# A decoder trunk in three-pass fp32r: two down-projections of each feed-forward stage turned from direct products into seven half-size products, and two of the four weight sums made by adding DMAs

## The reference, cut to what matters

```python
def swiglu_half(h, g, w1, w3, w2):
    u = rmsnorm(h, g)
    return h + 0.5 * ((jax.nn.silu(u @ w1) * (u @ w3)) @ w2)

def decoder_layer(h, ...):
    h = swiglu_half(h, *ffn1)
    h, sd, sq, sc = hybrid_mixer(h, s_delta, s_qkv, s_conv, n_lead, *mixp)
    h = swiglu_half(h, *ffn2)
    return h, sd, sq, sc
```

## Time and profile before

| | |
|---|---|
| median of 3 runs | 1204.9 us |
| the profiled execution | 1204.62 us |
| its span, first to last instruction | 1202.6 us |
| TensorE busy, matmuls | 1190.0 us (99%), 8832 |
| VectorE busy | 788.3 us (66%) |
| ScalarE busy | 515.5 us (43%) |
| POOL busy | 76.5 us (6%) |
| granted TensorE clock, mean | 0.997 of full speed |
| moved by DMA | 99.68 MB, mean 83 GB/s |

### The profile page before, as it was taken

How to read it: one execution, slowest core, us unless ns; L and a number is a source line. 1 busy time by engine, 2 the same in 40 slices (tenths; PEclk the granted TensorE clock), 3 DMA queues, 4 the chain that set the end, 5 groups by cost and what they waited for, 6 DMA issues and landing times.

```text
span 1202.6 us, 21067 instructions
## 1 busy us (share of the span) xinstructions
PE 1190.0 (99%) x8832; PEld 1162.1 (97%) x8832; DVE 788.3 (66%) x1155; ACT 515.5 (43%) x820; POOL 76.5 (6%) x58
## 2 busy tenths in 40 slices
PE   9999999999999999999999999999999999999997
PEld 9999999999999998999989898999999999999997
DVE  6887565767566633766557787547776667675764
ACT  6345343435344532433443444443344344353355
POOL 0000000000000300000125210220000000000003
PEclk9999999999999999999999999999999999999999
DMA  5321212221212422211510002422133121222112
GB/s 191 128 87 72 105 62 97 89 105 71 106 71 105 117 95 70 67 57 54 122 9 1 1 2 88 132 70 89 53 116 124 69 97 63 97 106 105 71 71 79
DMA packets 39212, 99.68 MB, mean 83 GB/s; under 512 B 12112, under 2 KB 15568, under 8 KB 39120
## 3 DMA queue, kind: packets, MB, share of 16 engines
q1 hardware_dynamic: 38064, 96.00, 23.4%
q10 hardware_dynamic: 1056, 2.36, 0.5%
HBM read 92.91 MB, written 5.44 MB: 82 GB/s over the span
## 4 chain that ended last, share of the span: by engine, by line
PE 92%; issue 3%; DVE 2%; ACT 1%; POOL 1%; DMA 0%; POOLq 0%; DVEq 0%; SPq 0%
PE ps L846 34%; PE ps L813 21%; PE ps L762 19%; PE ps L958 10%; PE ps L1349 4%; PE ps L726 1%; PE ps L1155 1%; PE ps L1363 1%; ACT x_hi L1431 1%; DVE w_lo L1926 1%; DVE h L1988 1%; PE ps L928 0%; PE ps L982 0%; PE ps L1261 0%; DMA h<-x_t 0%
## 5 line engine op out<-in xcount | busy, mean ns | idle before, releaser
L846 PE MATMUL ps<-x_hi,s_hi 128*128 128x296 f32 (+1 forms) x576 | 171.2, 297 | 0.2
L846 PE MATMUL ps<-x_hi,s_lo 128*128 128x296 f32 (+1 forms) x576 | 170.9, 297 | 0.0
L846 PE MATMUL ps<-x_lo,s_hi 128*128 128x296 f32 (+1 forms) x576 | 170.9, 297 | 0.0
L762 PE MATMUL ps<-x_hi,w_hi 128*128 128x296 f32 (+1 forms) x608 | 136.1, 305 | 0.3 <-DVE x_lo L1931 0.3
L762 PE MATMUL ps<-x_lo,w_hi 128*128 128x296 f32 (+1 forms) x608 | 131.8, 298 | 0.0
L762 PE MATMUL ps<-x_hi,w_lo 128*128 128x296 f32 (+1 forms) x608 | 131.7, 298 | 0.0
L846 PE MATMUL ps<-t_hi,s_hi 128*128 128x296 f32 (+1 forms) x432 | 128.3, 297 | 0.0
L846 PE MATMUL ps<-t_hi,s_lo 128*128 128x296 f32 (+1 forms) x432 | 128.1, 297 | 0.0
L846 PE MATMUL ps<-t_lo,s_hi 128*128 128x296 f32 (+1 forms) x432 | 128.0, 296 | 0.0
L2025 DVE TENSOR_TENSOR s_lo<-s_sum,s_hi 128x1024 fp32r<-128x1024 f32 x72 | 88.2, 1225 | 43.0 <-ACT s_hi L1418 40.3
L846 PEld LDWEIGHTS ps<-x_hi,s_hi 128*128 128x128 f32 x576 | 108.4, 188 | 0.6 <-issue 0.6
(11 more groups left out here) (322 smaller groups left out, 2556.4 us busy)
## 6 DMA issues: line engine op xcount, KB each, us to landing
raw<-weights SPq DMA_DIRECT2D x150, 512.0 KB, 3.3
raw<-weights SPq DMA_DIRECT2D x16, 384.0 KB, 3.5
S<-states SPq DMA_DIRECT2D x1, 2048.0 KB, 11.8
new_state<-S ACTq DMA_DIRECT2D x1, 2048.0 KB, 6.9
y_t<-h SPq DMA_DIRECT2D x4, 336.0 KB, 2.3
h<-x_t SPq DMA_DIRECT2D x4, 296.0 KB, 5.0
h<-x_t SPq DMA_DIRECT2D x2, 592.0 KB, 7.0
raw<-weights SPq DMA_DIRECT2D x4, 256.0 KB, 5.3
```

Of the source, the lines that this page charges most:

```text
L762: last = nc.tensor.matmul(ps[:, slot if out is None else out, half, 0:w_half], w[:, slot, k, :], x[:, k, a:a + w_half], start=(k == 0 and ...
L846: last = nc.tensor.matmul(out, w[:, k, :], x[:, k, :], start=(start and k == 0 and r == 0), stop=(k == KT // 2 - 1 and r == 2), skip_group ...
```

## The change: what it does

1. `PARTS` is `[4, 4, 4, 3, 3, 4]`. The parts of four tiles that are neither first nor last, parts 1 and 2 of each stage, are `split`.
2. The down-projection of a split part is done by the same seven products. A pair `j` of 0 to 3 is one 2 by 2 block product: two output tiles (2j, 2j+1) from two times two hidden tiles, with token halves as columns. One pair is seven products of 2 k-steps, 42 matmuls. The weights of pairs 0 and 1 are one use of the piece set (`pair_uses[0]`), those of pairs 2 and 3 the other (`pair_uses[1]`).
3. It needs T1 to T4 of the hidden tiles: tiles 0 and 1 keep their second token half aside and give T1; tiles 2 and 3 give T3, T2, T4 (`gt_sums`), each cast (`gt_cast`) and with its rest (`gt_rest`, `rests`).
4. `h` takes from each pair three adds in place of two: M7 alone on both halves, the rest of the second row, the first row.
5. S3 and S1 are no longer made on VectorE. SP loads one block in their place (`load_bases`) and POOL issues a DMA that adds the other block to it (`add_bases`, `accum_op=ALU.add`). S3 and S1 and what follows change sign, so the adds to `h` have -0.5.
6. In the mixer the first `w` of `ORDER` moves behind one step of `a` and two of `s`, `hist_q` is loaded after the masks, some semaphores are merged, and rows of `work` are 8 columns longer.

```diff
-PARTS = [4, 4, 3, 3, 4, 4]
+PARTS = [4, 4, 4, 3, 3, 4]
...
+        self.split = n == 4 and 0 < at < len(PARTS) - 1
...
-    "aabaabbsatazsaabaazbaabaabscaabtabasbaabsababaasbsstaassaaacansasaswasssshhhwssshww"
+    "aabaabbsatazsaabaazbaabaabscaabtabasbaabsababaasbsstaassaaacansasasasswsshhhwssshww"
...
+            def load_bases(t):                                   # SP
+                for i, at in enumerate((S3, S1)):
+                    sum_free(sp, t, at)
+                    if t.w or i:
+                        sp.wait_ge(base_in, 32 * t.w + 16 * i)
+                    sp.dma_start(piece(2, t.use, at), weights[t.u + 1][:, 0:KT // 2]).then_inc(base_in, 16)
...
+            def add_bases(stage):                                # POOL
+                for part in FFN[stage][1:]:
+                    for t in part.tiles + part.pair_uses:
+                        for i, (at, j, k) in enumerate(((S3, 0, 0), (S1, 1, KT // 2))):
+                            pool.wait_ge(base_in, 32 * t.w + 16 * (i + 1))
+                            if t.w or i:
+                                pool.wait_ge(base_sums, 32 * t.w + 16 * i)
+                            pool.dma_start(piece(2, t.use, at), weights[t.u + j][:, k:k + KT // 2],
+                                           accum_op=ALU.add).then_inc(base_sums, 16)
...
++            def down_sevenths(part):                             # TensorE
+                pair_m1(part, 1)
+                for j in range(2):
+                    for product_of in (pair_m7, pair_m6, pair_m2):
+                        product_of(part, j, (0,))
+                pair_m7(part, 0, (1,))
+                pair_m6(part, 0, (1,))
+                pair_m2(part, 0, (1,))
+                pair_m5_m4(part, 0)
+                pair_m7(part, 1, (1,))
+                pair_m6(part, 1, (1,))
+                pair_m2(part, 1, (1,))
+                pair_m3(part, 0)
+                pair_m5_m4(part, 1)
+                pair_m1(part, 2)
+                pair_m7(part, 2)
+                pair_m3(part, 1)
+                pair_m6(part, 2)             # waits for S2 of the second pair use, hi and lo
+                pair_m2(part, 2)
+                pair_m5_m4(part, 2)
+                pair_m1(part, 3)
+                pair_m7(part, 3)
+                pair_m3(part, 2)             # waits for pair_rest_add(2)
+                pair_m6(part, 3)
+                pair_m2(part, 3)
+                pair_m5_m4(part, 3)
+                m1(FFN[part.stage][part.at + 1].tiles[0])
+                pair_m3(part, 3)
...
+            def down_sevenths(part, lo):                         # ScalarE
+                hi_first(second)
+                pair_seed("b", part, 1)
+                first_casts(t, lo)
+                last_casts(t, lo)
+                pair_seed("c", part, 0)
+                hi_sums(second, 0)
+                pair_seed("c", part, 1)
+                hi_sums(second, 1)
+                hi_last(second)
+                pair_seed("b", part, 2)
+                hi_first(after)
+                pair_seed("c", part, 2)
+                hi_sums(after, 0)
+                pair_seed("b", part, 3)
+                hi_sums(after, 1)
+                pair_seed("c", part, 3)
+                seed(after)
+                hi_last(after)
...
+            def gt_sums(t, lo):                                  # VectorE
+                dve.wait_ge(halves_out, half_out("product", t.t))
+                dve.wait_ge(g_ready, G_DONE["T1", t.part.tiles[j].abs])
+                V.tensor_tensor(t3, b22, t3, ALU.subtract).then_inc(halves_out, 1)
+                V.scalar_tensor_tensor(t2, t2, -1.0, b22, ALU.mult, ALU.subtract).then_inc(halves_out, 1)
+                dve.wait_ge(halves_out, half_out("T2", t.t))
+                V.scalar_tensor_tensor(t4, t2, -1.0, b21, ALU.mult, ALU.subtract).then_inc(halves_out, 1)
...
+            def down_sevenths(part, lo):                         # VectorE
+                rests(t, lo)
+                lo_first(second)
+                pair_m7_add(part, 0)
+                pair_rest_add(part, 0)
+                sum_two(second)
+                lo_sums(second, 0)
+                pair_add(part, 0)
+                pair_m7_add(part, 1)
+                pair_rest_add(part, 1)       # waits for d4 of pair 1
+                sum_four(second)
+                lo_sums(second, 1)           # waits for the cast of S2 with S4
+                pair_add(part, 1)
+                lo_last(second)
+                lo_first(after)
+                pair_m7_add(part, 2)
+                sum_two(after)               # waits for the adding DMAs of the next part's first tile
+                pair_rest_add(part, 2)
+                lo_sums(after, 0)
+                sum_four(after)
+                pair_add(part, 2)
+                pair_m7_add(part, 3)
+                lo_sums(after, 1)
+                pair_rest_add(part, 3)
+                pair_add(part, 3)
+                lo_last(after)
```

More of the change, by code:

```diff
@@ L77, in __init__, with pair @@
         self.uses = 0 if at == 0 else n + 2
+        self.pair_uses = [PairUse(self, i) for i in range(2)] if self.split else []
+    def pair(self, j):
+        return self.stage, self.at, j
     def tile(self, i):
@@ L106, in __init__, with split_number @@
         self.use = part.use + i
+        self.w = split_number(part) + i
         self.last = i == part.n - 1
+class PairUse:
+    def __init__(self, part, i):
+        self.part, self.i = part, i
+        self.u = part.down + 2 * i
+        self.use = part.use + part.n + i
+        self.w = split_number(part) + part.n + i
+def split_number(part):
+    sizes = [n + 2 * (n == 4 and at < len(PARTS) - 1) for at, n in enumerate(PARTS) if at]
+    return part.stage * sum(sizes) + sum(sizes[:part.at - 1])
 def ffn_parts(stage):
@@ L666, in load_parts @@
                     for t in part.tiles:
-                        load_used(part, t.u, t.use, KT)
-                    for i in range(2):
+                        for load in (load_bases, load_tile) if t.use == 1 else (load_tile, load_bases):
+                            load(t)
+                    for x in part.pair_uses:
+                        load_tile(x)
+                        load_bases(x)
+                    for i in range(0 if part.split else 2):
                         load_used(part, part.down + 2 * i, part.use + part.n + i, 2 * part.n)
@@ new lines, in pair_m3, with down_sevenths @@
+            def pair_m3(part, j):
+                pe.wait_ge(halves_out, half_out("rest", part.pair(j)))
+                pair_seventh(part, j, S4, "B22", "c", False).then_inc(unit_done, part.step(2 * j) + part.step(2 * j + 1))
+            def down_sevenths(part):
+                pair_m1(part, 1)
+                for j in range(2):
+                    for product_of in (pair_m7, pair_m6, pair_m2):
[23 more added lines that the diff above has]
+                pair_m3(part, 3)
@@ L1524, in by_sevenths @@
                     hi_sums(nxt, 1)
-                    seed(nxt)
+                    if t.last:
+                        pair_seed("b", part, 0)
+                    else:
+                        seed(nxt)
                     hi_last(nxt)
@@ L2048, in by_sevenths @@
                 part, lo = t.part, lo_of(t.part.stage)
-                nxt = None if t.last else part.tiles[t.i + 1]
+                nxt = following(t)
                 if t.i:
```

400 lines of the change are left out of this document (330 added, 70 removed).

## The result

| | before | changed |
|---|---|---|
| median (4 runs each, side by side) | 1204.79 us | 1238.93 us |
| lowest to highest | 1204.36 to 1205.02 | 1237.25 to 1242.89 |
| ratio, 95% interval | | 1.0283 [1.0262, 1.0305] |
| profiled execution, its span | 1204.62, 1202.6 us | 1240.19, 1238.4 us |

The change makes the kernel 34 us slower. The forecast was 1205.6 us in a range of 1199 to 1218; the time lies outside it, on the side of rival 1.

The account below looks back on a forecast made before the run. TensorE, never idle in the feed-forward windows, was taken as the bound. Matmuls saved -12.9 us and new waits +13.6 net +0.7: 1204.6 becomes 1205.3, 1205.6 as a median; eight-in-ten range 1199 to 1218 us.

Parts of the forecast that it names:

- rival 1: Adding DMAs land late, x above 3.7 us, VectorE waits in `sum_two`; x of 4 to 5 gives 1208 to 1222; chance 0.32.
- 96 matmuls fewer: Four split down-projections, two per stage, each drop 24 matmuls, at 0.1359 and 0.1326 us each: 12.9 us saved.
- The waits of the split parts' own queues: TensorE's new waits for VectorE and ScalarE in split parts: 3.4 us a part, 13.6 for four.
- A: Split down-projection: m6 of pair 2 waits for S2, behind pair 1's rest add, sum, cast and rest: 2.0 us lost.
- B: m1 of pair 1, first product after the last tile's m4, waits for that tile's SiLU on ScalarE: 0.5 us lost.
- C: k-step 1 of pair 0 waits for T3 and g of the last tile: 0.5 us lost together.
- D: m5 of pair 3 waits for a seed behind ScalarE's cast of 1024 for the next part: 0.3 us lost.
- POOL is held up by a busy VectorE: GpSimd writes DMA descriptors in SBUF, and VectorE's two-port modes lock it out: 0.25 us or so a time.
- x: Time of one adding DMA from POOL's release to its semaphore: taken as 3.3 us, bounded by 2.7 and 5.3.
- 2.7 + 2x <= 10.1: Split part's end: a load and two serial adds must fit before the next part's `sum_two`; x up to 3.7 us.
- the forecast's own case: Adds in time, split parts lose 3.0 to 4.2 us each: net -0.9 to +3.9 us; chance 0.40.
- The moved `w`: Mixer, near 740 us: 1.06 us of ScalarE and 1.2 of VectorE move elsewhere; -1 to +1, taken as 0.

Follow-up runs that it names:

- experiment 1: Changed kernel without the 88 adding DMAs, SP's base load giving their signal (additions left out): 1209.77 us, ratio 1.0037 to the kernel before.
- experiment 5: experiment 1 with VectorE and ScalarE making S2 and S4 of the second pair use before waiting for pair 1: 1199.58 us, ratio 0.9952.
- experiment 9: Experiment 7 with S2 and S4 sums ahead of the activation rests in tiles 1 to 3 of split parts: 1198.61 us, ratio 0.9952.
- experiment 4: Changed kernel with POOL's 88 DMAs as plain copies in series, without the addition (sums left out): 1210.26 us, ratio 1.005.
- experiment 10: Changed kernel, adds in series, each covering only the first half of its block, 128 KB (other half left out): 1214.16 us, ratio 1.01.
- Experiment 7: Changed kernel with both adds of a use in flight, `w` back in place, and S2 and S4 made earlier in split down-projections: 1201.42 us, ratio 0.9978.
- experiment 3: Changed kernel with separate semaphores, so a use's two base loads and two adds no longer wait for each other: 1211.33 us, ratio 1.0059.

## Why the prediction was wrong

**What held.** 96 matmuls fewer, at the pitch of the earlier trace rows: starts on time follow each other after 0.136 us in stage 0 and 0.133 in stage 1 in both kernels, and the experiments that take the waits away shorten the stages. The waits of the split parts' own queues: 13.6 forecast, 13.1 measured in experiment 1, and not by chance, since they agree place by place: A 2.0 (2.0 forecast), B 0.4 to 0.5 (0.5), C 0.6 (0.5), D 0.15 to 0.3 (0.3). Chain A's four ops took 3.73 us (3.86). A and B are also shown by the edits that remove them, experiments 5 and 9; C and D were not tested apart.

**What did not.** The forecast would be wrong by much "if TensorE stands in the middle of tiles". It does: 9.3 us at L1009 for ScalarE, the largest row of its waits. VectorE at the end of a split part (134 to 160 us) is busy 20.7 of 26 us, 80% and not near 90%. And the reason for late adds that POOL is held up by a busy VectorE shows nowhere in POOL's issues: they took 0.865 us at the median and 1.01 at most over all 88.

**The step that failed: x.** "It reads 256 KB twice, so I take the row of 512 KB, 3.3." That was a row of SP's queue used for POOL's. Measured, x is 5.1 us at the median, near the upper bound of the text: POOL's 0.86 us of issuing, then some 4.2 until it is released. The plain copy of experiment 4 shows how it is made up: a transfer of this size on POOL's queue is already 4.1 with no addition (3.6 to landing, against 2.8 from SP); the addition brings 1.0 more, 0.33 of it on POOL. How much of the copy's time is due to the loads beside it no run here separates. The condition, 2.7 + 2x <= 10.1, was the right one, and rival 1 named place, mechanism and what would show it: VectorE in `sum_two` for a DMA, x from POOL's row. It was given 0.32 where the forecast had 0.40, and the range was cut at x = 4.9.

By the Trainium skill (DMA: Bandwidth & Descriptors, "Anatomy of one DMA") a DMA that GpSimd issues takes 2.0 us and its bytes at 436 GB/s, 2.6 for 256 KB; here the plain copy took 3.6 us to landing and 4.1 to the next release, the add 4.7 and 5.1. The measurement decides, and it was also the page's figure that made a value near 3.3 look safe.

**The second miss: the slope.** Even with x right the forecast would have been too low. For x = 5.3 the text had about +21 us over the forecast's own case, some 19 for 5.1. The changed kernel's waits are 20.6 + 24.8 = 45.4; less 13.1 of experiment 1 and 3.4 of granted clock (below) the late adds cost 28.9. It is also steeper: at x = 4.1 they cost 0.5 (experiment 4 against 1), or 4.4 in experiment 10, where the text had +3 to +4. The loss feeds itself: the use after the late one starts its load late too, and load, add, add took 16.6 us where the text had 11.8, with base loads of 5.0 and 3.8 us in the chain in place of 2.7. I had laid out the first late tile, not the loop.

**The moved `w`.** Taken as 0 (-1 to +1); it costs 2.0. In the changed kernel's mixer TensorE stands for the rest of that split:

```profile
760.13 1.22 DVE L2254 TENSOR_TENSOR w_lo<-raw,w_hi 128x1024 fp32r<-128x1024 f32 x1
...
761.40 0.53 PE L1523 MATMUL ps<-xoc_hi,w_hi 128*128 128x288 f32 x2 [1.97 <-DVE w_lo L2254]
```

ScalarE's cast of 1.04 us and VectorE's rest of 1.22 now lie behind two steps that TensorE waits for in turn, where one of them had covered it. Putting it back gave 1.7.

**The granted clock.** A new term. Stage 1 has two stretches where TensorE was granted less; the windows (clock is the number before the last two):

```profile
980.00:985.00 5.00, 3.05 (x15) 3.06 (x16) 3.32 (x5) 2.85 (x5) 0.88 (x1) 0.77 0.55 114
985.00:990.00 5.00, 5.00 (x36) 5.00 (x35) 4.29 (x8) 2.85 (x5) 0.88 (x1) 0.89 0.54 126
```

And TensorE's timeline there, after a wait of 2.26 us:

```profile
981.95 0.40 PE L1009 MATMUL ps<-x_hi,s_hi 128*128 128x288 f32 x1 [2.26 <-ACT up_gate L1796]
982.19 0.29 PE L1009 MATMUL ps<-x_lo,s_hi 128*128 128x288 f32 x1
...
983.18 0.44 PE L1009 MATMUL ps<-x_lo,s_hi 128*128 128x288 f32 x1
...
986.23 0.29 PE L1009 MATMUL ps<-x_hi,s_lo 128*128 128x288 f32 x1
```

From 982.7 to 986.1 the matmuls follow each other every 0.24 us in place of 0.13, the lower of the two levels (1.2 GHz), then the full one again. That stretch costs (0.23 + 0.11) x 5 = 1.7 us; the other (0.73 and 0.93, 1035 to 1045) as much: 3.4. Experiment 7, with short waits, has none in these stages. But a long wait does not always bring one: of experiment 1's four waits of 1.7 us one did, and experiment 10, with four such, has none in its stages. When it comes is open. The mixer has such a stretch too, one in the kernel before (630 to 640 us, 0.83) and a longer one in the changed kernel (645 to 660 us, 0.77), 1.7 us more.

**The sum again.** -12.9 + 13.1 (own waits) + 28.9 (late adds) + 3.4 (clock) + 3.0 (mixer: 2.0 `w`, 1.7 clock, less 0.7 not traced) = +35.5, where the spans differ by 35.8. This is no independent check, as 28.9 is what was left over; experiments 1 and 3 give the adds 29.2 and 27.6. The best version, experiment 9, saves 5.8 us in the two stages and not 12.9. Its rows of waits name some 2 us there; the starts more than 0.15 us apart show the rest, 8.1 us against 0.9 before: 3.2 at C, 3.6 where the next part's first tile begins, and small ones. Most are each under 0.4 us and so hardly leave idle time. C is thus the next place to mend, and it has been in the forecast from the start.

## What to carry to other kernels

Price a transfer by a row of the queue that will issue it; without one, the slowest row of its size is the value to plan with, and a step that fits only below it is a coin toss. Before a chain of load, transfer, transfer is laid into a loop, compare its whole length with what the loop leaves between the place coming free and the first use: above it the loss comes back at every turn, 2.4 us in two tiles here. And let two transfers that don't touch each other's bytes go without waiting for one another; here that alone was worth 28 us. Last, a list of waits is not a list of losses: where matmuls overlap in the record, look at the distance of their starts.

## What the runs showed of the hardware

- 256 KB from HBM to SBUF, in these kernels: 2.8 us to landing from SP's queue; from POOL's 3.6 as a plain copy and 4.7 as an add. POOL is held for 0.54 us by the copy and 0.86 by the add; from one issue to the next of a pair in series are 4.1 and 5.1 (medians of 44). An add of 128 KB takes 3.7 to landing and 4.0 to the next issue.
- Two adds issued within 1.1 us of each other (13 pairs of experiment 3) landed after 3.8 and 5.3 us at the median, the second 5.9 after the first was issued; in series that took 10.6.
- A matmul record here is 0.30 us long while the next starts 0.136 after it (296 columns), so a start that is late by up to 0.16 us shows as no idle time.
- `scalar_tensor_tensor` on two float32 operands in SBUF costs what `tensor_tensor` does. VectorE in stage 0 of the changed kernel (line, shape, count, busy us, mean ns):

```profile
L2277 DVE TENSOR_TENSOR gt_sum<-up_gate,gt_sum 128x296 f32<-128x296 f32 x4 | 1.9, 467 | 0.1
L2278 DVE SCALAR_TENSOR_TENSOR gt_sum<-gt_sum,up_gate 128x296 f32<-128x296 f32 x4 | 1.8, 460 | 0.0
```

The row decided rightly over the rule on it that the prediction weighed from the Trainium skill (Vector Engine (DVE) Microarchitecture Reference, "Points that are easy to get wrong").
